# A two-layer encoder on one core: first norm's weights loaded by themselves, x's operands rounded straight from x, first weight bases split by DMA

## The chip, the cores and the metric

The kernel runs on one NeuronCore of one Trainium2 chip. The metric is the device time of one execution in microseconds (us). All work is float32. TensorE multiplies operands of type fp32r, a rounded float32; to keep the precision each operand is split into a high part (the value rounded to fp32r) and a low part (the value less its high part), and each product is made as high x high, high x low and low x high: three matmuls where one would do.

## What is computed

Two layers of a Conformer-like trunk over 528 tokens (16 meta tokens and 512 of the sequence), width 1024. Only the first part of the first layer matters here:

```
x = x + 1/2 * SwiGLU_1(RMSNorm(x))          # ffn1_norm, ffn1_w_in, ffn1_w_out
h = RMSNorm(x); proj = h @ w_in             # conv branch | attention | gates
x = x + W_out(sigmoid(g_A) * y_A + sigmoid(g_B) * y_B)
x = x + 1/2 * SwiGLU_2(RMSNorm(x))

def rms_norm(x, g):
    return x * rsqrt(mean(x * x) + EPS) * g
def swiglu(h, w_in, w_out):
    gu = h @ w_in
    gate, up = gu[..., :D_FF], gu[..., D_FF:]
    return (silu(gate) * up) @ w_out
```

## The kernel before

Everything is kept transposed: features on the 128 partitions, tokens along the free axis. x is `resid`, eight blocks (m = 0 to 7) of 128 features by 528 tokens.

**The product of an FFN's first stage.** The 2816 gate and 2816 up columns are cut into 22 "pairs" j, each 128 gate and 128 up columns. A pair is multiplied by a Strassen-like scheme in seven products P1 to P7 instead of eight. `seventh` (L1125) makes one product: 12 matmuls of 264 columns, in steps kp = 0 to 3. The other side of the products are seven operands made from two x blocks at a time (m = 2kp and 2kp + 1, each in halves of 264 tokens, times the norm's weight): B11, B21, B22 are such halves themselves, and T1 to T4 are sums and differences of them. Their high parts stand in `x7h`, their low parts in `x7l`. A pair's weights arrive in `raw` (SyncE's queue, `load_pair`: 768 KB, then 256 KB). Of them two tiles ("A", 128x1024) and one tile ("A22", 128x512) are used as they are: these are the **bases**. Four more tiles are sums (`sum12`, `sum43`), which VectorE adds. High parts of weights are in `wha`/`whb`, low parts in `wla`/`wlb`.

**How weights are split.** Sums, in all pairs, are rounded on ScalarE (`sum_hi`, L709) and subtracted on VectorE (`sum_lo`, L1537). The bases of pairs 2 and up: ScalarE rounds (`base_hi`, L687; `base22_hi`, L698) and writes the negative of the rounded part into the low buffer (L691, L702), and then a DMA on GpSimd's queue adds the weights from memory onto it (`accum_op=ALU.add`, L617 and L622). The bases of pair 0 and A of pair 1 are rounded on ScalarE too, but subtracted on VectorE (`first_base_lo`, L1553), which counts `first_lo`; A22 of pair 1 goes the way of the later ones.

**The order of work at the begin.** Each engine has its instructions in an order written out by hand, and waits on semaphores. ScalarE issues the loads of all parameters (`prm`, 312 KB, L668, and two small ones), waits for them, and then goes through the x blocks (`x7_parts`): L758 writes x times the weight as float32 into a scratch buffer (`tmp` or a part of `ga`), L769 squares x for the norm's statistic, L766 and L772 round the operands. VectorE (`x7_operands`) makes the sums T1 to T4 from the scratch (L1494 to L1503) and the low parts (L1489). TensorE waits for the first base (`first_lo`), then alternates between the statistic (`first_stat`, L1145: a product of ones with the squares, four records a block) and P1's steps; after that come P2, P5, P6, P3 of pair 0 and P1, P2 of pair 1. The squares have four buffers, so that the square of block m > 3 waits until the statistic of block m - 4 is done (`sq_used`). After the opening ScalarE copies banks (L724, L729, L734) and VectorE takes the gate sum (`gate_sum`, L1626) of pair 0, and goes on with pair 1's sums.

Of the kernel before, what the change touches and what calls it, by code (L numbers as in the profile page):

```python
# [25 lines left out]
ACT = mybir.ActivationFunctionType  # L26
# [237 lines left out]
def build(nc, x, params, qk_gain, sinks, pairs, outs6, outs5, mixes, out):  # L264
# [7 lines left out]
    with ctx:  # L272
# [26 lines left out]
        gnext = sb("gnext", [P, KD])  # L299
        qk = sb("qk", [HD, 4])  # L300
# [163 lines left out]
        prm_in, first_lo, sq_used = sem("prm_in"), sem("first_lo"), sem("sq_used")  # L464
# [74 lines left out]
        def _(sp):  # L539
# [4 lines left out]
            def load_pair(j):  # L544

                j0, j1 = run_of(j)
                if j - 2 >= j0:
                    sp.wait_ge(a_hi, j - 1)
                    sp.wait_ge(s_sum, 4 * (j - 1))
                if j in (2, 3):  # L550

                    sp.wait_ge(first_lo, 2 * j - 3)
                sp.dma_start(raw[:, j % 2, KP:4 * KP, :], pairs[j, :, KP:4 * KP, :]).then_inc(raw_in[j % 2], 16)
                if j - 2 >= j0:
                    sp.wait_ge(a22_hi, j - 1)
                if j == 2:
                    sp.wait_ge(first_lo, 2)
                sp.dma_start(raw[:, j % 2, 0:KP, :], pairs[j, :, 0:KP, :]).then_inc(raw22_in[j % 2], 16)
# [26 lines left out]
            load_pair(1)  # L585
            for l in range(DEPTH):
# [26 lines left out]


# [50 lines left out]
        def _(act):  # L665
            func = nc.scalar.activation

            act.dma_start(prm[:, :, :], params).then_inc(prm_in, 16)  # L668
            act.dma_start(qk[:, :], qk_gain).then_inc(par_in, 16)
            act.dma_start(sink[:, :, :, :], sinks).then_inc(par_in, 16)  # L670
# [10 lines left out]
            def base_hi(j):  # L681
# [6 lines left out]
                if j < 2:  # L688
                    return
                act.wait_ge(a_hi, j + 1)  # L690
                func(units(lo_units, U_A[REGION[j]], 2), hi.bitcast(F32), ACT.Copy, scale=-1.0).then_inc(a_neg, 1)  # L691

            def base22_hi(j):
# [5 lines left out]
                if j == 0:  # L699
                    return  # L700
                act.wait_ge(a22_hi, j + 1)
# [44 lines left out]

            def x7_parts(l, which, s, m, gain):
# [6 lines left out]
                if s:  # L754
                    act.wait_ge(acc_done, (n - 1) * (KD + 2) + m + 1)
                if m > (1 if s else 3):
                    act.wait_ge(x7_lo, X7_PARTS * (k - (s == 0)) - 1)
                func(tmp[:, 3 * w:5 * w] if odd else tmp[:, 6 * w:8 * w], resid[:, m, a:], ACT.Identity,  # L758
                     scale=gain).then_inc(b_done, 1)
                if odd:  # L760
                    act.wait_ge(b_done, s * KD + m + 1)

                    n = 2 if s else 4
                    if s == 0:
                        act.wait_ge(t_step, 4 * k + 1)
                    func(x7h[:, kp, 0:n * w], tmp[:, 3 * w:(3 + n) * w], ACT.Copy).then_inc(x7_hi, n // 2)  # L766
                if s == 0 and m > 3:
                    act.wait_ge(sq_used, m - 3)
                func(sq_m[:, m % 2, a:] if s else first_sq(m), resid[:, m, a:], ACT.Square).then_inc(x_sq, 1)  # L769
# [3 lines left out]
                elif s:  # L773
                    act.wait_ge(t_step, 4 * k + 1)
                    func(x7h[:, kp, 2 * w:4 * w], tmp[:, 5 * w:7 * w], ACT.Copy).then_inc(x7_hi, 1)
# [112 lines left out]
            act.wait_ge(prm_in, 16)  # L888
            for m in range(KD):
                act.wait_ge(x_in[m], 16)  # L890
                x7_parts(0, 0, 0, m, prm[:, m, R_FFN1 * DEPTH:R_FFN1 * DEPTH + 1])
                if m == 1:
                    base_hi(0)
                if m == 3:
                    base22_hi(0)
                if m == 5:
                    sum_hi(0, 0)
            sum_hi(0, 1)
            base_hi(1)
# [191 lines left out]
        def _(pe):  # L1091
# [67 lines left out]
            def last_product(j):  # L1159
                pe.wait_ge(*((a22_lo[j % 2], 16 * ((j + 1) // 2)) if j else (first_lo, 2)))  # L1160
# [21 lines left out]
            def ffn(l, f):  # L1182
                s, which = 2 * l + f, 2 * f
                for c, (ta, tb) in enumerate(CHUNKS):
# [10 lines left out]
                    for j in range(j0, j1):  # L1195
# [6 lines left out]
                        pe.wait_ge(*((a_lo[j % 2], 16 * (j // 2)) if j > 1 else (first_lo, 2 * j + 1)))  # L1202
# [244 lines left out]
        def _(dve):  # L1447
# [27 lines left out]

            def x7_operands(l, which, s, m):
# [16 lines left out]
                if not odd:  # L1493
                    tt(t1, b11, b12, ALU.subtract).then_inc(t_step, 1)  # L1494
                    if s:
                        add_squares(n, m, a)
                        low(1, T1, 5, 2)
# [6 lines left out]
                low(2, B21, 3, 2 if s else 4)  # L1504
                if s:
                    add_squares(n, m, a)
# [49 lines left out]
            for k in range(KD):  # L1556
                x7_operands(0, 0, 0, k)
                if k == 1:
                    first_base_lo("A", 0)
                if k == 3:  # L1560
                    sum12(0)
                    sum43(0)
                if k == 5:
                    sum_lo(0, 0)
            sum_lo(0, 1)
            first_base_lo("A22", 0)
            first_base_lo("A", 1)
# [437 lines left out]
def laid_out(inputs):  # L2005
# [12 lines left out]
    for l in range(DEPTH):  # L2018
# [11 lines left out]
    return {  # L2030
        "x": tiles(np.concatenate([f["meta_tokens"], f["x"][0]])),
# [24 lines left out]
```

## Time and profile before

| | before |
|---|---|
| median of 3 runs | 2352.43 us |
| lowest and highest | 2347.88 and 2353.43 us |
| profiled execution, its own time | 2354.66 us |
| its span | 2352.8 us |
| TensorE busy | 2319.3 us, 99% of the span |
| VectorE, ScalarE, GpSimd busy | 71%, 53%, 15% |
| granted TensorE clock, mean | 0.999 |

The span is the time between the first and the last instruction of the profile; the profiled execution took 1.9 us more than its span. Every slice of a fortieth of the span but the first shows TensorE at 90% or more.

### The profile page before, as it was taken

The page shows a single profiled execution, that of the slowest core. Times are in us where ns is not written, and L with a number is a line of the kernel's source. Part 1 is how long each engine was busy: PE and PEld are TensorE (multiplying, and loading weights), DVE is VectorE, ACT ScalarE, POOL GpSimd, SP SyncE. Part 2 cuts the span into 40 slices and gives each one's busy share as a digit, 9 for nine tenths or more (in the row PEclk, how much of TensorE's full clock was granted, in tenths as well). Part 3 has the DMA queues.
Part 4 walks back from the last instruction along what each step waited for, and adds up shares of the span by engine and source line. Part 5 has one row for each costly group of instructions (what it writes and reads, how often), then busy time and mean ns, then how long its engine had stood idle before and what let it go on. Part 6 is the DMA issues. An engine that isn't in the chain of part 4 may idle for free.

```text
span 2352.8 us, 43248 instructions
## 1 busy us (share of the span) xinstructions
PE 2319.3 (99%) x17765; PEld 2202.2 (94%) x17765; DVE 1678.4 (71%) x2751; ACT 1246.6 (53%) x2023; POOL 345.9 (15%) x454
## 2 busy tenths in 40 slices
PE   7999999999999999999999999999999999999999
PEld 6999999999999999999999999999888777998997
DVE  8855854899995488568677558548999755874773
ACT  8734734454445486356577357344544455862751
POOL 1101101112112211011011011012122122110110
PEclk9999999999999999999999999999999999999999
DMA  6845736677768968467458467366777698773753
GB/s 179 183 121 140 172 93 149 150 155 157 149 136 206 205 140 180 113 147 181 117 139 186 113 146 170 88 152 150 163 163 152 136 220 186 161 181 102 171 132 110
DMA packets 111365, 358.71 MB, mean 152 GB/s; under 512 B 12608, under 2 KB 12608, under 8 KB 111168
## 3 DMA queue, kind: packets, MB, share of 16 engines
q0 software_dynamic: 64080, 210.53, 44.1%
q1 hardware_dynamic: 46720, 145.08, 21.2%
q8 instruction: 141, 2.31, 0.4%
q14 instruction: 56, 0.46, 0.1%
q10 hardware_dynamic: 368, 0.33, 0.0%
HBM read 351.41 MB, written 2.10 MB: 150 GB/s over the span
## 4 chain that ended last, share of the span: by engine, by line
PE 83%; DVE 8%; DMA 4%; ACT 3%; issue 2%; DVEq 0%; ACTq 0%; SPq 0%
PE po L1108 26%; PE po L1125 21%; PE po L1176 21%; PE ptr L1125 7%; PE pov L1125 5%; DVE cv L1776 3%; DMA wha<-in_mixes 1%; DMA raw<-in_pairs 1%; DMA wla<-in_mixes 1%; PE pov L1368 1%; PE pov L1371 1%; PE pstat L1328 1%; DVE t L1817 1%; PE ptr L1337 1%; ACT whb L687 0%
## 5 line engine op out<-in xcount | busy, mean ns | idle before, releaser
L1108 PE MATMUL po<-xh,wha 128*128 128x264 f32 (+1 forms) x1408 | 346.9, 313 | 2.1 <-DMA wla<-in_mixes 1.6
L1108 PE MATMUL po<-xl,wha 128*128 128x264 f32 (+1 forms) x1408 | 335.8, 305 | 0.0
L1108 PE MATMUL po<-xh,wla 128*128 128x264 f32 (+1 forms) x1408 | 335.1, 305 | 0.0
L1776 DVE SCALAR_TENSOR_TENSOR cv<-ub,lp,cv 128x528 f32<-128x528 f32 (+1 forms) x480 | 333.2, 752 | 1.7
L1176 PE MATMUL po<-hh,wla 128*128 128x264 f32 (+1 forms) x1232 | 283.8, 300 | 0.0
L1176 PE MATMUL po<-hl,wha 128*128 128x264 f32 (+1 forms) x1232 | 283.7, 300 | 0.0
L1176 PE MATMUL po<-hh,wha 128*128 128x264 f32 (+1 forms) x1232 | 282.5, 299 | 0.4 <-DVE wla L1545 0.4
L678 ACT ACTIVATE wla<-wha 128x1024 fp32r<-128x1024 f32 x136 | 143.8, 1059 | 231.2 <-DMA wha<-in_mixes 231.0
L1545 DVE TENSOR_TENSOR wla<-wfa,wha 128x768 fp32r<-128x768 f32 (+1 forms) x128 | 113.8, 890 | 203.8 <-ACT wha L716 203.7
L1108 PEld LDWEIGHTS po<-xh,wha 128*128 128x128 f32 x1408 | 227.1, 189 | 24.3 <-issue 7.3
L716 ACT ACTIVATE wha<-wfa 128x768 fp32r<-128x768 f32 (+1 forms) x128 | 101.0, 789 | 268.8 <-DMA wfa<-in_outs 268.7
L1108 PEld LDWEIGHTS po<-xh,wla 128*128 128x128 f32 x1408 | 226.5, 188 | 11.2
L1108 PEld LDWEIGHTS po<-xl,wha 128*128 128x128 f32 x1408 | 226.9, 188 | 9.8
L1125 PE MATMUL po<-x7h,wha 128*128 128x264 f32 (+1 forms) x832 | 236.0, 284 | 0.0
L1125 PE MATMUL po<-x7h,wla 128*128 128x264 f32 (+1 forms) x832 | 236.0, 284 | 0.0
L1125 PE MATMUL po<-x7l,wha 128*128 128x264 f32 (+1 forms) x832 | 236.0, 284 | 0.0
L1125 PE MATMUL po<-x7h,whb 128*128 128x264 f32 (+1 forms) x768 | 220.5, 287 | 6.3 <-ACT tmp L729 3.4
L1125 PE MATMUL po<-x7l,whb 128*128 128x264 f32 (+1 forms) x768 | 218.2, 284 | 0.0
L1125 PE MATMUL po<-x7h,wlb 128*128 128x264 f32 (+1 forms) x768 | 217.7, 283 | 0.0
L1176 PEld LDWEIGHTS po<-hh,wha 128*128 128x128 f32 x1232 | 196.1, 188 | 8.5 <-DVE wla L1545 0.6
L1176 PEld LDWEIGHTS po<-hh,wla 128*128 128x128 f32 x1232 | 196.9, 189 | 7.5
L1176 PEld LDWEIGHTS po<-hl,wha 128*128 128x128 f32 x1232 | 196.4, 188 | 7.5
(251 smaller groups left out, 5659.1 us busy)
## 6 DMA issues: line engine op xcount, KB each, us to landing
wha<-in_mixes POOLq DMA_DIRECT2D x136, 512.0 KB, 4.4
wla<-in_mixes POOLq DMA_DIRECT2D x136, 512.0 KB, 6.8
raw<-in_pairs SPq DMA_DIRECT2D x88, 768.0 KB, 5.6
wfa<-in_outs SPq DMA_DIRECT2D x64, 384.0 KB, 3.1
wlb<-in_pairs POOLq DMA_DIRECT2D x47, 512.0 KB, 8.4
raw<-in_pairs SPq DMA_DIRECT2D x88, 256.0 KB, 6.9
wla<-in_pairs POOLq DMA_DIRECT2D x87, 256.0 KB, 6.6
wfa<-in_outs SPq DMA_DIRECT2D x64, 320.0 KB, 2.9
```

What stands on the lines that cost most here:

```text
L678: func(mix_units(lo_units, n), mix_units(hi_units, n).bitcast(F32), ACT.Copy, scale=-1.0)\
L716: func(units(hi_units, u, 2)[:, 0:k, :], units(f32_units, u, 2)[:, 0:k, :], ACT.Copy).then_inc(ob_hi, 1)
L1108: ins = mm(po[:, 2 * out_slot + h, 0:width], w[:, k, :], v[:, k, t:t + width], start=begin and k == 0 and p == 0, stop=last and k == kt - ...
L1125: ins = mm(bank, a[:, kp, :], b[:, kp, cols7], start=begin and kp == 0 and p == 0, stop=kp == KP - 1 and p == 2, skip_group_check=True)
L1176: ins = mm(po[:, 2 * ps(m) + h, 0:width], w[:, k, :], v[:, t, x:x + width], start=t == 0 and p == 0, stop=t == CHUNK_T - 1 and p == 2, ski ...
L1328: ins = mm(score(i, h), q[r, :], kw[r, c:c + WK], start=True, stop=True)
L1337: ins = tr(ptr[:, (2 * n + h) * P:(2 * n + h + 1) * P], pw[:, (b + 1) % 2, at:at + WIN], ident[:, :])
L1368: mm(dst[h * HD:(h + 1) * HD], vw[:, pos - 1, :], cut(pt[:, i, h, :]), start=True, stop=False, skip_group_check=True)
L1371: ins = mm(dst[h * HD:(h + 1) * HD], vz[0:n, i - i0, h, :], cut(ptm[0:n, :]), start=pos == 0, stop=True, skip_group_check=True)
L1545: tt(units(lo_units, u, 2)[:, 0:k, :], units(f32_units, u, 2)[:, 0:k, :], units(hi_units, u, 2)[:, 0:k, :].bitcast(F32), ALU.subtract).the ...
L1776: stt(cv[:, j, a:], u, w, cv[:, j, a:], ALU.mult, ALU.add).then_inc(conv_step, 1)
L1817: nc.vector.reciprocal(t0[0:HD, :], t0[0:HD, :]).then_inc(krms_ready, 1)
```

## The change

It touches the first some thirty microseconds of the program, and nothing after pair 3's loads. (1) The first norm's weight is an input of its own, `first_gain`, 128x8 elements; ScalarE loads it first, and the loads of all parameters move to SyncE's queue, behind pair 1's. (2) `x7_parts` and `x7_operands` give way, in the first stage, to `first_parts` and `first_operands`: B11, B21 and B22 are rounded straight from `resid` with the weight as scale, without a copy in the scratch (only B12 is written there), and VectorE takes their low parts and the sums from `resid` too, with a negated weight `nfgain`. (3) The bases of pair 0 and A of pair 1 are not rounded on ScalarE or subtracted on VectorE: a DMA on GpSimd's queue loads the weights into the high buffer, rounding on the way (`first_load`), ScalarE writes the negative (`first_base_neg`), and a second DMA adds the weights (`first_add`). (4) SyncE's waits for pairs 2 and 3 drop what hung on `first_lo`.

```
+            firsts = ((0, U_A, 2, KP, 3 * KP), (0, U_A22, 1, 0, KP), (1, U_A, 2, KP, 3 * KP))
+            def first_load(i):
+                j, u, n, a, z = firsts[i]
+                pool.dma_start(units(hi_units, u[REGION[j]], n), pairs[j, :, a:z, :]).then_inc(first_hi[i], 16)
+            def first_add(i):
+                j, u, n, a, z = firsts[i]
+                pool.wait_ge(first_neg, i + 1)
+                pool.dma_start(units(lo_units, u[REGION[j]], n), pairs[j, :, a:z, :], accum_op=ALU.add)\
+                    .then_inc(first_lo[i], 16)
+            first_load(0)
+            pool.wait_ge(x_in[3], 16)
+            first_load(1)
+            first_add(0)
+            pool.wait_ge(x_in[6], 16)
+            first_load(2)
+            first_add(1)
+            first_add(2)
...
-            act.dma_start(prm[:, :, :], params).then_inc(prm_in, 16)
-            act.dma_start(qk[:, :], qk_gain).then_inc(par_in, 16)
-            act.dma_start(sink[:, :, :, :], sinks).then_inc(par_in, 16)
+            act.dma_start(fgain[:, :, :], first_gain).then_inc(gain_in, 16)
...
+            def first_base_neg(i):
+                j, u, n = ((0, U_A, 2), (0, U_A22, 1), (1, U_A, 2))[i]
+                act.wait_ge(first_hi[i], 16)
+                func(units(lo_units, u[REGION[j]], n), units(hi_units, u[REGION[j]], n).bitcast(F32), ACT.Copy,
+                     scale=-1.0).then_inc(first_neg, 1)
+            def first_squares(m):
+                if m > 3:
+                    act.wait_ge(sq_used, m - 3)
+                func(first_sq(m), resid[:, m, :], ACT.Square).then_inc(x_sq, 1)
+            def first_parts(kp):
+                tmp, w = x7_scratch(0, kp), NH
+                e, o = 2 * kp, 2 * kp + 1
+                act.wait_ge(x_in[e], 16)
+                if kp > 1:
+                    act.wait_ge(x7_lo, X7_PARTS * (kp - 1) - 1)
+                func(tmp[:, 7 * w:8 * w], resid[:, e, w:2 * w], ACT.Identity, scale=fgain[:, e, :]).then_inc(b_done, 2)
+                func(x7h[:, kp, B11 * w:(B11 + 1) * w], resid[:, e, 0:w], ACT.Identity, scale=fgain[:, e, :])
+                first_squares(e)
+                act.wait_ge(t_step, 4 * kp + 1)
+                func(x7h[:, kp, T1 * w:(T1 + 1) * w], tmp[:, 5 * w:6 * w], ACT.Copy).then_inc(x7_hi, 1)
...
-            act.wait_ge(prm_in, 16)
...
+            act.wait_ge(gain_in, 16)
+            first_parts(0)
+            first_base_neg(0)
+            first_parts(1)
+            first_base_neg(1)
+            first_parts(2)
+            sum_hi(0, 0)
+            first_parts(3)
             sum_hi(0, 1)
-            base_hi(1)
+            first_base_neg(2)
...
-                        pe.wait_ge(*((a_lo[j % 2], 16 * (j // 2)) if j > 1 else (first_lo, 2 * j + 1)))
+                        pe.wait_ge(*((a_lo[j % 2], 16 * (j // 2)) if j > 1 else (first_lo[2 * j], 16)))
...
-            def first_base_lo(part, j):
-                a, z, first_unit, n = (KP, 3 * KP, U_A, 2) if part == "A" else (0, KP, U_A22, 1)
-                dve.wait_ge(a_hi if part == "A" else a22_hi, j + 1)
-                u = first_unit[REGION[j]]
-                tt(units(lo_units, u, n), raw[:, j, a:z, :], units(hi_units, u, n).bitcast(F32), ALU.subtract)\
-                    .then_inc(first_lo, 1)
```

GpSimd's queue, from its last instruction of the constants on. Before:

```order
L610 AFFINE_SELECT ident<-ident 128x128
L617 DMA wlb<-in_pairs 128x1024 [waits a_neg]
L622 DMA wla<-in_pairs 128x512 [waits a22_neg]
L617 DMA wla<-in_pairs 128x1024 [waits a_neg]
L622 DMA wla<-in_pairs 128x512 [waits a22_neg]
```

And with the change:

```order
L613 AFFINE_SELECT ident<-ident 128x128
L622 DMA whb<-in_pairs 128x1024
L622 DMA wha<-in_pairs 128x512 [waits x_in3]
L627 DMA wlb<-in_pairs 128x1024 [waits first_neg]
L622 DMA wha<-in_pairs 128x1024 [waits x_in6]
L627 DMA wla<-in_pairs 128x512 [waits first_neg]
L627 DMA wla<-in_pairs 128x1024 [waits first_neg]
L641 DMA wlb<-in_pairs 128x1024 [waits a_neg]
L646 DMA wla<-in_pairs 128x512 [waits a22_neg]
```

Six transfers now stand ahead of pair 2's addition. The one that ends in `wlb` is pair 0's A, behind the load of A22, which waits for x block 3; the last `first_neg` one is pair 1's A.

ScalarE, from the first use of x blocks 2 and 3 to the negative or rounding of A22. Before:

```order
L687 ACTIVATE whb<-raw 128x1024 [waits raw_in0]
L758 ACTIVATE ga<-resid,prm 128x528 [waits x_in2]
L769 ACTIVATE ga<-resid 128x528
L758 ACTIVATE ga<-resid,prm 128x528 [waits x_in3]
L766 ACTIVATE x7h<-ga 128x1056 [waits t_step,b_done]
L769 ACTIVATE ga<-resid 128x528
L772 ACTIVATE x7h<-ga 128x792 [waits t_step]
L698 ACTIVATE wha<-raw 128x512 [waits raw22_in0]
```

And with the change:

```order
L768 ACTIVATE wlb<-whb 128x1024 [waits first_hi0]
L783 ACTIVATE ga<-resid,fgain 128x264 [waits x_in2]
L784 ACTIVATE x7h<-resid,fgain 128x264
L774 ACTIVATE ga<-resid 128x528
L787 ACTIVATE x7h<-ga 128x264 [waits t_step]
L789 ACTIVATE x7h<-resid,fgain 128x528 [waits x_in3]
L774 ACTIVATE ga<-resid 128x528
L793 ACTIVATE x7h<-ga 128x792 [waits t_step]
L768 ACTIVATE wla<-wha 128x512 [waits first_hi1]
```

The two full-width copies into the scratch became one of half the width, and the instruction on the weights reads what a DMA wrote instead of `raw`.

ScalarE, from block 7's square on to the first bank copy. Before:

```order
L769 ACTIVATE ga<-resid 128x528 [waits sq_used]
L772 ACTIVATE x7h<-ga 128x792 [waits t_step]
L709 ACTIVATE whb<-wfb 128x1024 [waits s_sum]
L687 ACTIVATE wha<-raw 128x1024 [waits raw_in1]
L724 ACTIVATE tmp<-po 128x264 [waits t_step,c12_taken,blk_used]
```

And with the change:

```order
L774 ACTIVATE ga<-resid 128x528 [waits sq_used]
L793 ACTIVATE x7h<-ga 128x792 [waits t_step]
L727 ACTIVATE whb<-wfb 128x1024 [waits s_sum]
L768 ACTIVATE wla<-wha 128x1024 [waits first_hi2]
L742 ACTIVATE tmp<-po 128x264 [waits t_step,c12_taken,blk_used]
```

The negative of pair 1's A stands in the place of its rounding, at the end of the opening, and the addition of pair 1's A waits for it.

## Rows read from the trace of the kernel before

**Rows 1.** Busy time by stretches: opening, two pairs, rest, first transfers.

```profile
0.00:11.45 11.45, 0.67 (x4) 0.62 (x4) 5.36 (x13) 8.01 (x12) 0.91 (x9) 1.00 0.86 305
11.45:31.20 19.75, 17.46 (x91) 14.72 (x92) 18.97 (x29) 17.73 (x25) 0.00 (x0) 1.00 0.32 108
31.20:52.90 21.70, 19.82 (x160) 19.24 (x158) 21.23 (x32) 17.66 (x26) 3.75 (x5) 1.00 0.71 160
52.90:2352.80 2299.90, 2281.37 (x17514) 2167.61 (x17514) 1632.84 (x2680) 1203.20 (x1963) 341.26 (x441) 1.00 0.66 152
4.00:14.00 10.00, 2.55 (x6) 2.04 (x7) 7.38 (x12) 8.99 (x13) 0.00 (x0) 1.00 1.03 400
```

**Rows 2.** Timeline of TensorE: start, duration, idle before with its releaser.

```profile
11.45 3.89 PE L1145 MATMUL pstat<-ga,ones 128*128 128x264 f32 x8 [9.00 <-DVE wlb L1553]
...
15.69 1.94 PE L1145 MATMUL pstat<-ga,ones 128*128 128x264 f32 x8
...
20.17 1.16 PE L1145 MATMUL pstat<-ga,ones 128*128 128x264 f32 x4 [1.28 <-ACT ga L769]
...
28.28 0.39 PE L1125 MATMUL po<-x7h,whb 128*128 128x264 f32 x1 [0.67 <-ACT tmp L724]
...
35.14 0.36 PE L1125 MATMUL po<-x7h,whb 128*128 128x264 f32 x1 [0.73 <-DVE tmp L1630]
...
49.31 0.39 PE L1125 MATMUL po<-x7h,whb 128*128 128x264 f32 x1 [0.74 <-ACT tmp L724]
...
52.89 0.36 PE L1125 MATMUL po<-x7h,whb 128*128 128x264 f32 x1 [0.40 <-ACT tmp L729]
```

**Rows 3.** Timeline of ScalarE, the same columns.

```profile
4.84 0.73 ACT L758 ACTIVATE tmp<-resid,prm 128x528 f32<-128x528 f32 x1 [0.96 <-DMA prm<-in_params]
5.48 0.63 ACT L769 ACTIVATE ga<-resid 128x528 f32<-128x528 f32 x1
...
8.34 0.85 ACT L772 ACTIVATE x7h<-tmp 128x792 fp32r<-128x792 f32 x1
9.09 1.04 ACT L687 ACTIVATE whb<-raw 128x1024 fp32r<-128x1024 f32 x1
10.04 0.72 ACT L758 ACTIVATE ga<-resid,prm 128x528 f32<-128x528 f32 x1
...
26.91 1.04 ACT L687 ACTIVATE wha<-raw 128x1024 fp32r<-128x1024 f32 x1
27.86 0.37 ACT L724 ACTIVATE tmp<-po 128x264 f32<-128x264 f32 x1
```

**Rows 4.** Timeline of VectorE, the same columns.

```profile
28.18 1.82 DVE L1553 TENSOR_TENSOR wla<-raw,wha 128x512 fp32r<-128x512 f32 x2
29.92 0.43 DVE L1626 TENSOR_TENSOR tmp<-pov,tmp 128x264 f32<-128x264 f32 x1
```

**Rows 5.** The issues of x blocks 2 and 3: duration, first and last start, landing.

```profile
L542 SPq DMA_DIRECT2D resid<-in_x x2: 480/568/657, 2.6 to 3.3; - x2
...
DMA to landing us min/median/max: 6.4/6.4/6.4
```

**Rows 6.** Adding transfers of 512 KB, whole run: issue ns, landing.

```profile
L617 POOL DMA_DIRECT2D wlb<-in_pairs x47: 861/866/1014, 32.9 to 2261.4; - x47
L617 POOL DMA_DIRECT2D wla<-in_pairs x39: 859/866/889, 47.0 to 2251.7; - x39
...
DMA to landing us min/median/max: 5.4/8.5/12.0
```

**Rows 7.** The first of them, issued at 32.9, in the same columns.

```profile
L617 POOL DMA_DIRECT2D wlb<-in_pairs x1: 1014/1014/1014, 32.9 to 32.9; - x1
...
DMA to landing us min/median/max: 8.6/8.6/8.6
```

**Rows 8.** The mixer's plain rounding loads of 512 KB, whole run.

```profile
L627 POOL DMA_DIRECT2D wha<-in_mixes x136: 543/546/868, 320.0 to 1979.4; - x136
...
DMA to landing us min/median/max: 3.7/4.4/9.4
```

More of the change, by code:

```diff
@@ L261, in block_source, with build @@
     return "w_in", (({A: 0, B: O_B, GA: O_GA, GB: O_GB}[kind] + j * P, P),)
-def build(nc, x, params, qk_gain, sinks, pairs, outs6, outs5, mixes, out):
+def build(nc, first_gain, x, params, qk_gain, sinks, pairs, outs6, outs5, mixes, out):
     rows = lambda w: w.rearrange("l (k p) n -> p l k n", p=P)
@@ L463, in build @@
         raw_in, raw22_in = [sem(f"raw_in{s}") for s in range(2)], [sem(f"raw22_in{s}") for s in range(2)]
-        prm_in, first_lo, sq_used = sem("prm_in"), sem("first_lo"), sem("sq_used")
+        prm_in, sq_used = sem("prm_in"), sem("sq_used")
+        gain_in, gain_neg = sem("gain_in"), sem("gain_neg")
+        first_hi, first_lo = [sem(f"first_hi{i}") for i in range(3)], [sem(f"first_lo{i}") for i in range(3)]
+        first_neg = sem("first_neg")
         a_hi, a_neg, a_lo = sem("a_hi"), sem("a_neg"), [sem(f"a_lo{s}") for s in range(2)]
@@ L585, in _ @@
             load_pair(1)
+            sp.dma_start(prm[:, :, :], params).then_inc(prm_in, 16)
+            sp.dma_start(qk[:, :], qk_gain).then_inc(par_in, 16)
+            sp.dma_start(sink[:, :, :, :], sinks).then_inc(par_in, 16)
             for l in range(DEPTH):
@@ L761, in x7_parts @@
                     act.wait_ge(b_done, s * KD + m + 1)
[L763 to L769, printed above, removed]
+                    func(x7h[:, kp, 0:2 * w], tmp[:, 3 * w:5 * w], ACT.Copy).then_inc(x7_hi, 1)
+                func(sq_m[:, m % 2, a:], resid[:, m, a:], ACT.Square).then_inc(x_sq, 1)
                 if odd:
@@ L1494, in x7_operands @@
                     tt(t1, b11, b12, ALU.subtract).then_inc(t_step, 1)
-                    if s:
-                        add_squares(n, m, a)
-                        low(1, T1, 5, 2)
+                    add_squares(n, m, a)
+                    low(1, T1, 5, 2)
                     return
@@ L1503, in x7_operands @@
                 stt(t4, t2, -1.0, b21, ALU.mult, ALU.subtract).then_inc(t_step, 1)
-                low(2, B21, 3, 2 if s else 4)
-                if s:
-                    add_squares(n, m, a)
+                low(2, B21, 3, 2)
+                add_squares(n, m, a)
                 low(3, T3, 0, 3)
@@ L1546, in out_lo @@
                    units(hi_units, u, 2)[:, 0:k, :].bitcast(F32), ALU.subtract).then_inc(ob_lo, 1)
-            def first_base_lo(part, j):
-                a, z, first_unit, n = (KP, 3 * KP, U_A, 2) if part == "A" else (0, KP, U_A22, 1)
-                dve.wait_ge(a_hi if part == "A" else a22_hi, j + 1)
-                u = first_unit[REGION[j]]
-                tt(units(lo_units, u, n), raw[:, j, a:z, :], units(hi_units, u, n).bitcast(F32), ALU.subtract)\
-                    .then_inc(first_lo, 1)
[L1556 to L1564, printed above, removed]
+            dve.wait_ge(gain_in, 16)
+            ts(nfgain[:, :, :], fgain[:, :, :], -1.0, None, ALU.mult).then_inc(gain_neg, 1)
+            dve.wait_ge(gain_neg, 1)
+            first_operands(0)
+            first_operands(1)
+            sum12(0)
+            sum43(0)
+            first_operands(2)
+            sum_lo(0, 0)
+            first_operands(3)
             sum_lo(0, 1)
-            first_base_lo("A22", 0)
-            first_base_lo("A", 1)
             def layer_params(l):
```

68 lines of the change are left out of this document (40 added, 28 removed).

## The prediction

> **What bounds the kernel now.** I read the busy time by stretches first, then the timelines of TensorE, ScalarE and VectorE over the opening, then the transfers. TensorE is busy 2281.4 of the 2299.9 us after 52.9 [rows 1]; nothing of the change reaches there, so the question is only when TensorE comes to the point that it reaches at 52.9 now. Before that it has 0.67 + 17.46 + 19.82 us of work [rows 1] and a begin at 11.45, when VectorE has subtracted the first base [rows 2]. From there the reader is to see two things. First, TensorE has idle time of 2.3 us up to 31.2 (19.75 less 17.46) and 1.9 us more in three waits, 0.73, 0.74 and 0.40, up to 52.9 [rows 1, 2], because ScalarE and VectorE feed it just in time: ScalarE works without a gap from 26.91 to its bank copy at 27.86 [rows 3], and VectorE takes the gate sum at 29.92 only because the last two base subtractions fill 28.18 to 30.0 [rows 4]. Second, the transfers are the busiest part of the begin: from 4 to 14 us they move 400 GB/s at a busy share of 1.03 [rows 1]. So a gain would have to come from the 11.45 us of the start or the 4.2 us of idle; the whole stake is a few us of 2352.
>
> **What the change removes.** (a) ScalarE's wait for the parameters, 0.96 us before 4.84 [rows 3]. It can begin at 3.9 at the earliest, as its table load and constant end there, and it needs x block 0; I take 4.3, a gain of 0.5. (b) ScalarE's work per pair of x blocks. Now it takes 4.25 us (4.84 to 9.09, rounding of the base not included) [rows 3]. After: two 264-wide pieces at some 0.4, two squares at 0.54 (the distance of the starts; one lasts 0.63), a 264-wide copy 0.3 (the bank copy lasts 0.37), a 528-wide piece 0.64, the 792-wide copy 0.75, together 3.5 to 3.6. Four times 0.7 is 2.8 us. (c) On VectorE the base subtractions: 1.2 us after the first pair (as one half of L1553's kind) and the 1.8 at 28.18 [rows 4], 3 us; its sums and low parts cost the same, cut differently. These gains are real only where ScalarE and VectorE set the pace.
>
> **What it adds, and this decides.** TensorE's begin waited for a subtraction; now it waits for a chain through GpSimd's queue. All of TensorE's opening is queued behind that one wait: the statistic, P1, and through the four buffers of the squares ScalarE's block 4 and all behind it.
> - The load of pair 0's A goes out at about 1.7. The mixer's loads of that size land after 3.7 to 9.4 us, median 4.4 [rows 8]; so it lands at 6 to 11. ScalarE is done with pair 0 of x at 4.3 + 3.5 = 7.8; the negative (1.06, as the rounding of that size) ends at 9 to 12.
> - But the addition stands behind the load of A22, which waits for x block 3. That was issued at 3.3 and landed 6.4 later, at 9.7 [rows 5]. In flight ahead of it are now 512 KB more and 312 KB fewer; 0.2 MB at 400 GB/s is 0.5 us: 10.2. The A22 load's issue takes 0.87 (as each on that queue [rows 6]): the addition goes out at 11.1.
> - It lands 5.4 to 12.0 us later, median 8.5 [rows 6]; the first one of the run, issued while a pair's load was in flight, took 8.6 [rows 7]. At 11.1 some 1.5 to 2 MB of SyncE's transfers are still to come, so the quiet end, 5.4, is unlikely. I take 8.6: **T0 = 19.7**, against 11.45.
>
> The Trainium skill's page "DMA: Bandwidth & Descriptors" ("Anatomy of one DMA — SWDGE (gpsimd) path") gives a transfer from this queue as about 2.0 us plus the bytes at 436 GB/s. For 512 KB that would be 3.2 us, and T0 = 14.3. No row of this kernel comes near it: the fastest addition of 86 took 5.4 [rows 6], and not one plain load of 136 under 3.7 [rows 8].
>
> **From T0 on.** TensorE needs 17.5 us of work to the first product of pair 1 (busy time of 11.45 to 31.2 [rows 1]; its eight slow first records, 3.89 against 1.94 for the next eight [rows 2], are in it and stay, as it is idle before). Are its operands there? Pairs 0 and 1 of x are ready before T0. For the rest ScalarE waits until the statistic of block 0 is done, four slow records, T0 + 1.95. Then: square 0.54, copy 0.3, 0.64, to T0 + 3.45; block 5's square after the statistic of block 1 at T0 + 3.9; 0.54, 0.75, the rounded sum 0.95: T0 + 6.15. Pair 3: 3.6, and 0.4 for VectorE's first sum, which stands behind a low part: T0 + 10.15; second sum: 11.1; the negative of pair 1's A: T0 + 12.2. VectorE ends half a us behind the sum. TensorE needs pair 3's operands at T0 + 13, so it runs without the old 2.3 us of idle.
>
> Pair 1's A is the next thing late: its addition goes out at T0 + 12.2 and TensorE wants it at T0 + 17.5. At 32 us pair 2 has landed and pair 3 is not asked for, so the queue is quiet; between 5.4 and 8.6 I take 6: T0 + 18.2 = 37.9, a wait of 0.7, and the product starts 6.7 us later than at 31.2. If it takes 8.6, the wait is 3.3.
>
> Up to 52.9 the old waits of 1.9 us can give some back: 4.8 later. But the chain over ScalarE and VectorE, which made these waits, is late as well. P2 of pair 0 is done 2.9 us (P6, P3) before T0 + 17.5, the bank copies take 0.4 to 0.7, so the gate sum comes at T0 + 15.1 = 34.8, 4.9 later than 29.92. Behind the copies ScalarE has its table load and square root (2 us), which ended under VectorE's work before and now half come after it: some 0.5. Both ways give 4.8 to 5.4. **Sum: 5.4 us later**, all of it at the begin. The profiled execution took 2354.66, and would take 2360.1; the median of the runs is 2.2 lower, so 2357.8.
>
> The edits at nothing: the parameters' load behind pair 1's is wanted only by the layer's parameters, which VectorE takes among the first output blocks, behind eleven pairs; the work of these hides it, and it would cost only if it came later than they end. SyncE's dropped waits bring pair 2's A22 some 12 us earlier, which nobody waits for. The negated weight is eight elements on VectorE, under 0.2 us, before x.
>
> **The rivals.**
> - *As forecast*, T0 at 17.5 to 20.7: 2 to 7 us later. Chance 0.55.
> - *The transfers crowd each other more.* The addition takes 9.8 to 12, or x block 3 lands at 11 to 12 because two queues share the engines, or pair 1's addition takes the full 8.6 too. The last alone adds 2.6 less what the idle time takes, 1.5; each us of the first two adds one. 7.1 to 10 us later, 2359.5 to 2362. For it speaks that 4 to 14 us are full already [rows 1]; against it that x's first blocks are already out. Chance 0.24.
> - *The additions are quick*, 3.2 to 5.4 (the page's rule, or the lowest of [rows 6]): T0 = 14.3 to 16.5. Then all is shifted 5.4 to 3.2 less: 0 to 2.2 us later, 2352.4 to 2354.6. Chance 0.14.
> - *Faster*: the lighter opening of ScalarE and VectorE decides. That needs T0 under 14.3, the point where 2.9 us of later begin is paid by the 2.3 idle and 0.5 of the gate sum. With T0 at 12.5 it is 1.8 us faster, 2350.6; the most that ScalarE's 3.3 and VectorE's 3 us allow is 3 to 4. Against it stands that the addition goes out at 11.1 by block 3's landing alone, so it would have to land in 1.4 to 3 us. Chance 0.07, nearly all of it within 0.3%.
>
> **How the numbers follow.** 0.3%, 7.1 us here, is about what a measurement of this kernel can tell from no change; its three runs lie 5.5 us apart. The likeliest is 2357.8; its own range is 2354.4 to 2359.5. With the crowded case up to 10 us and half of the quick one, and the spread of the median by one or two us, the range for 8 in 10 is 2352.0 to 2361.8. Slower by over 0.3% is the crowded case, 0.24; faster by over 0.3% would need a gain beyond the whole idle time, 0.03; the rest, 0.73, is within.
>
> **What would show it.** In the changed profile: TensorE's first statistic at 18 to 21, released by the addition into `wlb` (step T0); ScalarE's square of block 4 waiting several us for TensorE (the buffers); TensorE without waits of over 0.5 us from there to pair 1, then a wait at its first product for a transfer into `wla` (0.7); the gate sum at 34 to 36; and the steady stretch beginning at 57 to 59 instead of 52.9. It is wrong if the addition lands within 5 us, if x block 3 lands well before 9.7, or if a wait remains behind 60 us that is not in the old trace.

## The result: 5.2 to 9.6 us slower, all of it at the begin

| | before | after |
|---|---|---|
| median of six runs each | 2352.2 us | 2360.67 us |
| lowest and highest | 2347.88 and 2353.43 | 2357.28 and 2364.96 |
| ratio after/before, 95% interval | | 1.0032 (1.0022 to 1.0041) |
| profiled execution, its own time | 2354.66 us | 2361.2 us |
| its span | 2352.8 us | 2359.4 us |
| TensorE busy | 2319.3 us, 99% | 2320.2 us, 98% |
| VectorE busy | 1678.4 us | 1678.0 us |

The interval is 5.2 to 9.6 us of 2352.2 us. The spans of the profiled executions lie 6.6 us apart and their times 6.5. Here is the changed kernel's busy time by stretches, in the columns of [rows 1]: stretch, length, busy time and count of TensorE, its weight loads, VectorE, ScalarE and GpSimd, then the granted TensorE clock, the transfers' busy share and GB/s.

```profile
0.00:21.55 21.55, 0.67 (x4) 0.61 (x4) 13.07 (x30) 11.34 (x20) 4.47 (x14) 1.00 0.95 306
21.55:39.59 18.04, 17.50 (x93) 15.43 (x93) 12.21 (x20) 13.61 (x21) 0.87 (x1) 1.00 0.41 94
39.59:59.37 19.78, 19.30 (x156) 19.11 (x157) 19.07 (x29) 16.95 (x25) 3.58 (x5) 1.00 0.77 176
59.37:2359.40 2300.03, 2282.70 (x17514) 2169.34 (x17514) 1633.66 (x2679) 1203.04 (x1963) 340.83 (x441) 1.00 0.66 152
4.00:14.00 10.00, 0.00 (x0) 0.00 (x0) 5.97 (x13) 6.91 (x14) 1.46 (x2) 1.00 1.01 357
```

The row to read first is the fourth. From 59.37 to the end it is 2300.03 us; before, from 52.9 to the end, it was 2299.90 [rows 1]. In these two executions the program behind the begin took the same time within 0.2 us, and the 6.5 us by which 52.89 became 59.37 are all but 0.1 us of the difference of the spans. The second row is the opening from TensorE's first statistic to the first product of pair 1: 17.50 us of work in 18.04 us, where before it was 17.46 in 19.75. The idle time is gone, but the stretch begins 10.1 us later.

TensorE's timeline (start, duration, instruction, in brackets the idle time before it and what released it) has three rows that count:

```profile
21.55 3.89 PE L1185 MATMUL pstat<-ga,ones 128*128 128x264 f32 x8 [19.10 <-DMA wlb<-in_pairs]
...
39.59 0.39 PE L1165 MATMUL ptr<-x7h,wha 128*128 128x264 f32 x1 [0.54 <-DMA wla<-in_pairs]
...
59.37 0.36 PE L1165 MATMUL po<-x7h,whb 128*128 128x264 f32 x1 [0.48 <-DVE wla L1598]
```

They answer to 11.45, 31.2 and 52.89 in [rows 1, 2]. The first release is no longer a subtraction on VectorE but a transfer into `wlb`, and the second is a transfer into `wla`. GpSimd's timeline shows what they hang on:

```profile
1.92 0.70 POOL L622 DMA_DIRECT2D whb<-in_pairs  x1 [0.24 <-issue]
12.42 0.54 POOL L622 DMA_DIRECT2D wha<-in_pairs  x1 [9.80 <-DMA resid<-in_x]
12.95 0.92 POOL L627 DMA_DIRECT2D wlb<-in_pairs  x1
...
34.04 0.87 POOL L627 DMA_DIRECT2D wla<-in_pairs  x1 [14.05 <-ACT wla L768]
```

The addition of pair 0's A stands behind the load of A22, and this behind the 9.80 us for x block 3. ScalarE, the same view:

```profile
3.74 0.51 ACT L783 ACTIVATE tmp<-resid,fgain 128x264 f32<-128x264 f32 x1 [1.05 <-DMA fgain<-in_first_gain]
...
10.37 1.06 ACT L768 ACTIVATE wlb<-whb 128x1024 fp32r<-128x1024 f32 x1 [2.95 <-DMA whb<-in_pairs]
...
23.71 0.64 ACT L774 ACTIVATE ga<-resid 128x528 f32<-128x528 f32 x1 [4.07 <-PE pstat L1185]
...
32.70 1.04 ACT L768 ACTIVATE wla<-wha 128x1024 fp32r<-128x1024 f32 x1
```

ScalarE begins 1.1 us earlier than before, and then stands 2.95 us for the load and 4.07 us for TensorE, which has not freed the squares' buffers. Last, the issues of x blocks 2 and 3, in the columns of [rows 5], and then the addition into `wlb`, in those of [rows 7]:

```profile
L546 SPq DMA_DIRECT2D resid<-in_x x2: 432/449/466, 2.6 to 3.1; - x2
...
DMA to landing us min/median/max: 8.9/9.0/9.0
```

```profile
L627 POOL DMA_DIRECT2D wlb<-in_pairs x1: 923/923/923, 13.0 to 13.0; - x1
...
DMA to landing us min/median/max: 8.6/8.6/8.6
```

The addition took the 8.6 us that were forecast. Block 3 did not land as forecast: it was issued at 3.1 and landed 9.0 us later, at 12.1 and not at 10.2.

### The profile page after: what moved, and what is told of

It reads as the page before. It is cut to its first block, busy times and chain, and to the rows that moved or that the text cites. A ratio compares the mean times of both kernels' runs of the same rounds, so it can differ in the third digit from the quotient of the medians.

```text
span 2359.4 us, 43254 instructions
## 1 busy us (share of the span) xinstructions
PE 2320.2 (98%) x17765; PEld 2204.5 (93%) x17765; DVE 1678.0 (71%) x2757; ACT 1244.9 (53%) x2027; POOL 349.7 (15%) x460
## 4 chain that ended last, share of the span: by engine, by line
PE 83%; DVE 8%; DMA 4%; ACT 3%; issue 2%; SPq 0%; POOL 0%; DVEq 0%; ACTq 0%
PE po L1148 25%; PE po L1165 22%; PE po L1216 21%; PE ptr L1165 7%; PE pov L1165 5%; DVE cv L1828 3%; DMA wha<-in_mixes 1%; DMA wla<-in_mixes 1%; PE pov L1408 1%; PE pov L1411 1%; PE pstat L1368 1%; DVE t L1869 1%; PE ptr L1377 1%; ACT pw L950 0%; ACT wla L700 0%
```

## The experiments

All times by label stand in one table. "First" is TensorE's first statistic, "gate" the start of VectorE's gate sum of pair 0, "last wait" the start of the instruction behind the last wait of the opening (52.89 before), "rest" the span less that, "raw A" the time from the issue of SyncE's load of pair 0's A (at 1.7) to its landing, "GB/s" what all transfers moved from 4 to 8 us. The ratio of each experiment is taken to runs of the kernel before from the same rounds, whose medians were 2353.54 us (e1 to e4), 2353.10 (e5 to e8) and 2354.18 (e9), and not to the 2352.2 of the first row.

| kernel | first | gate | last wait | rest | raw A | GB/s | median, us | ratio to before (95%) |
|---|---|---|---|---|---|---|---|---|
| before | 11.45 | 29.92 | 52.89 | 2299.9 | 6.0 | 383 | 2352.2 | |
| after | 21.55 | 36.16 | 59.37 | 2300.0 | 7.9 | 304 | 2360.67 | 1.0032 (1.0022 to 1.0041) |
| e1_old_split | 11.65 | 30.37 | 53.03 | 2299.8 | 7.6 | 253 | 2354.61 | 1.0004 (0.9995 to 1.0013) |
| e2_only_split | 19.86 | 33.50 | 60.57 | 2301.4 | 6.9 | 372 | 2359.58 | 1.0026 (1.0016 to 1.0036) |
| e3_add_first | 19.98 | 34.41 | 58.17 | 2302.2 | 8.6 | 291 | 2361.48 | 1.0033 (1.002 to 1.0045) |
| e4_stat_first | 5.20 | 34.87 | 57.88 | 2299.5 | 8.6 | 248 | 2359.2 | 1.0021 (1.0012 to 1.0029) |
| e5_prm_act | 10.22 | 28.95 | 51.61 | 2304.6 | 6.1 | 387 | 2352.95 | 1.0002 (0.9993 to 1.0011) |
| e6_mixed | 11.26 | 28.83 | 51.49 | 2302.5 | 7.2 | 291 | 2353.14 | 0.9997 (0.9987 to 1.0006) |
| e7_mixed_prm_act | 10.30 | 27.86 | 50.54 | 2300.6 | 5.9 | 388 | 2352.16 | 0.9997 (0.9988 to 1.0006) |
| e8_weight_alone | 11.46 | 30.35 | 53.34 | 2301.4 | 7.4 | 263 | 2355.58 | 1.001 (1.0001 to 1.0019) |
| e9_x_act | 10.99 | 28.55 | 51.22 | 2302.4 | 6.9 | 374 | 2354.96 | 1.0004 (0.9995 to 1.0014) |

Two columns help to read the others. The rest goes from 2299.5 to 2304.6 us by the profiled execution, over instructions that no edit touched; so the time of one execution cannot tell two kernels 2 us apart, and the ratios, with intervals 4 us wide, hardly can, and the begin is judged by the columns up to "last wait". These and the next two come from one execution of each kernel. How far they can be trusted is seen where two kernels run the same program up to 8 us: e1 and e6 read 7.6 and 7.2 us for raw A and 253 and 291 GB/s, and the changed kernel, e3 and e4 read 7.9, 8.6 and 8.6 us and 304, 291 and 248 GB/s. And from the gate sum to the last wait it is 22.7 to 23.8 us in all kernels but e2. What counts is when VectorE takes the gate sum.

### e1: the change with the old way of splitting

```
-            first_load(0)
...
-            first_add(2)
...
+                src = raw[:, j, 0:KP, :] if i == 1 else raw[:, j, KP:3 * KP, :]
+                func(units(hi_units, u[REGION[j]], n), src, ACT.Copy).then_inc(first_neg, 1)
...
             first_operands(0)
+            first_base_lo(0)
...
             sum_lo(0, 1)
+            first_base_lo(1)
+            first_base_lo(2)
```

ScalarE rounds the three bases from `raw` again and VectorE subtracts; parts (1) and (2) of the change stay.

> The changed kernel with its DMA split of the three first bases undone: ScalarE rounds them from raw and VectorE subtracts, as before; the weight by itself and the operands straight from x stay. If the additions on GpSimd's queue are the whole loss (my theory), TensorE begins at about 10 us instead of 21.6, and the gain of the rest of the change appears: VectorE, with some 23.7 us of work from 4.4 on, comes to its gate sum at about 28 instead of 29.9, and TensorE's steady stretch begins near 51 (52.9 before, 59.4 with the change); time 1 to 3 us under before. If the operands straight from x are a loss of their own (the rival), the steady stretch begins after 53 and the time is not under before.

The last wait ends at 53.03, 6.3 us before that of the changed kernel. So the split by transfers is what costs. But the other half of the expectation failed, and its rival's sign, a steady stretch after 53, is there: the rest of the change, which takes some 2.3 us of work off ScalarE (pair 0 of x takes 3.68 us instead of 4.25, four times), brings nothing (53.03 against 52.89). TensorE begins at 11.65 and not at 10, since the raw weights land 1.6 us later than before; e5 takes that up. For the work behind it VectorE shows the reason. First e1 from its first subtraction to the gate sum, then the low parts in e1's opening grouped by shape (count, busy time, mean ns of one, idle time before):

```profile
10.38:30.37 19.99, 16.88 (x83) 14.22 (x84) 19.81 (x33) 16.58 (x29) 0.00 (x0) 1.00 0.39 144
```

```profile
L1531 DVE SCALAR_TENSOR_TENSOR x7l<-resid,fgain,x7h 128x528 fp32r<-128x528 f32 x4 | 3.0, 762 | 0.0
...
L1528 DVE SCALAR_TENSOR_TENSOR x7l<-resid,fgain,x7h 128x264 fp32r<-128x264 f32 x4 | 2.0, 489 | 0.0
...
L1520 DVE SCALAR_TENSOR_TENSOR tmp<-resid,fgain,tmp 128x264 f32<-128x264 f32 x2 | 1.0, 490 | 0.5 <-ACT tmp L779 0.5
...
L1529 DVE TENSOR_TENSOR x7l<-tmp,x7h 128x264 fp32r<-128x264 f32 x2 | 0.9, 426 | 0.0
```

And the kernel before over the same piece, and its low parts and sums by shape:

```profile
10.17:29.92 19.75, 16.18 (x81) 13.44 (x82) 19.00 (x29) 17.73 (x26) 0.00 (x0) 1.00 0.35 123
```

```profile
L1489 DVE TENSOR_TENSOR x7l<-tmp,x7h 128x1056 fp32r<-128x1056 f32 x2 | 2.5, 1260 | 0.1
...
L1494 DVE TENSOR_TENSOR tmp<-tmp 128x264 f32<-128x264 f32 x2 | 0.9, 429 | 4.3 <-ACT tmp L758 4.3
```

VectorE is busy 19.81 of 19.99 us in e1: it sets the length of this piece, and ScalarE's lighter work buys nothing. Nor did VectorE itself get lighter. Per pair of x blocks its four sums took 4 x 0.43 and the first low part 1.26, 2.98 us. Now the sums take 4 x 0.49 (they multiply by the weight on the way), and that low part is cut in three, 0.49 + 0.43 + 0.76: 3.64 us. The 0.66 us more, four times, are 2.6 us, which is what the changed kernel gave back of the 3.1 us of the three subtractions it dropped. Its total says so: 1678.0 us against 1678.4.

### e2: the kernel before with the split alone

```
+            first_load(0)
+            pool.wait_ge(x_in[3], 16)
+            first_load(1)
+            first_add(0)
+            pool.wait_ge(x_in[6], 16)
+            first_load(2)
+            first_add(1)
+            first_add(2)
...
-                    base_hi(0)
+                    first_base_neg(0)
...
-                    first_base_lo("A", 0)
```

> The kernel before with the DMA split of the three first bases alone. If the additions are the whole loss, TensorE's first statistic comes at 21.5 to 22.5 and the steady stretch begins at 59 to 61, 6 to 8 us over before. If part of the loss comes from the operands straight from x, it begins at 56 or earlier.

The split alone puts the last wait 7.7 us later (60.57), and the total does not contradict it (1.0026, up to 1.0036). TensorE's timeline:

```profile
19.86 3.88 PE L1166 MATMUL pstat<-ga,ones 128*128 128x264 f32 x8 [17.42 <-DMA wlb<-in_pairs]
...
39.26 0.39 PE L1146 MATMUL ptr<-x7h,wha 128*128 128x264 f32 x1 [2.86 <-DMA wla<-in_pairs]
```

It begins 1.7 us before the changed kernel, and before the 21.5 that was expected (block 3 landed at 11.4, and the addition took 7.6 us). The wait for pair 1's A, 2.86 us, takes most of this back: it is the second wait for a transfer that the forecast named, and pair 1 starts at 39.26, still 0.3 us before the changed kernel's 39.59. From there to the last wait, however, it is 21.31 us instead of 19.78. This is the clock. Behind the long wait the matmuls start 0.12 us apart up to 40.6 and then 0.22 us apart up to 44.0, fifteen of them, 1.5 us more than at full speed, and the row of this stretch shows a granted clock of half:

```profile
40.90:44.00 3.10, 3.10 (x16) 3.10 (x15) 1.49 (x3) 2.78 (x4) 0.86 (x1) 0.50 0.91 170
```

In the changed kernel, which waited 0.54 us there, and in e3, which waited 1.08, the same piece takes 19.78 and 19.77 us. So a transfer that TensorE waits for can cost more than the wait.

### e3: the first addition ahead of A22's load

```
             first_load(0)
+            first_add(0)
             pool.wait_ge(x_in[3], 16)
             first_load(1)
-            first_add(0)
```

> The changed kernel with the addition onto pair 0's A issued before the load of A22, so that it does not wait for x block 3. If every us of the addition's landing is a us of the end, it goes out at 11.5 instead of 12.95, lands after the same 8.6, TensorE begins at 20.1 and the steady stretch at 57.9 instead of 59.4. If the transfers in flight set the landing and not the issue (rival), the addition takes as much longer as it goes out earlier, and nothing moves.

The addition now waits only for the negative, and goes out at 11.86 instead of 12.95:

```profile
11.86 0.87 POOL L627 DMA_DIRECT2D wlb<-in_pairs  x1 [9.25 <-ACT wlb L768]
```

The first statistic came 1.57 us earlier and the last wait ended 1.2 us earlier; pair 1's A took 0.5 back (a wait of 1.08 instead of 0.54). So the queue's order costs about 1 us, and most of the loss is the addition itself, which took 8.1 us here. The rival, that the landing would not move, is out. The total (1.0033) cannot tell this from the changed kernel.

### e4: the statistic before the wait for the base

```
-                        pe.wait_ge(*((a_lo[j % 2], 16 * (j // 2)) if j > 1 else (first_lo[2 * j], 16)))
+                        if j:
+                            pe.wait_ge(*((a_lo[j % 2], 16 * (j // 2)) if j > 1 else (first_lo[2], 16)))
...
                                     first_stat(2 * kp + 1)
+                                    if kp == 0:
+                                        pe.wait_ge(first_lo[0], 16)
```

> The changed kernel with TensorE's wait for pair 0's A moved behind the statistic of x blocks 0 and 1. If TensorE's work behind T0 is what the begin consists of, its 3.9 us of slow first statistic fall into the wait, and the steady stretch begins near 55.5 instead of 59.4; ScalarE's square of block 4 then waits for nothing. If the slow records only move to the products behind the wait, as TensorE is idle again for 10 us, a part of the 3.9, up to 2, is not gained.

The first eight statistic records left the chain, and ScalarE's square of block 4 waits for nothing, as expected; but the last wait ends only 1.5 us earlier, at 57.88, less than the 2 us that the expectation left at the worst. TensorE's timeline behind its wait:

```profile
21.88 0.59 PE L1165 MATMUL po<-x7h,whb 128*128 128x264 f32 x1 [12.80 <-DMA wlb<-in_pairs]
22.27 0.42 PE L1165 MATMUL po<-x7l,whb 128*128 128x264 f32 x1
22.49 0.42 PE L1165 MATMUL po<-x7h,wlb 128*128 128x264 f32 x1
22.71 3.72 PE L1185 MATMUL pstat<-ga,ones 128*128 128x264 f32 x8
...
29.34 0.29 PE L1165 MATMUL po<-x7l,whb 128*128 128x264 f32 x1
29.47 0.29 PE L1165 MATMUL po<-x7h,wlb 128*128 128x264 f32 x1
```

At 22.27 the matmuls start 0.22 us apart, at 29.34 0.13. 264 columns in 0.22 us is 1.2 GHz, the lower of the clock's two levels. TensorE had stood idle for 12.80 us before. Starting the statistic early did not spare the slow stretch, it made a second one: eight records took 3.89 us at 5.20 and the next eight 3.72 at 22.71, where the changed kernel's second eight take 2.64. The first product starts 2.98 us earlier than there (21.88 against 24.86), and the last step of P1 is done only 1.29 us earlier (29.59 against 30.88, the start of `pov`).

### e5 and e8: where the parameters' load stands

e5 is e1 with the parameters' loads back on ScalarE's queue, behind the first weight's; e8 is the kernel before with part (1) of the change alone.

```
             act.dma_start(fgain[:, :, :], first_gain).then_inc(gain_in, 16)
+            act.dma_start(prm[:, :, :], params).then_inc(prm_in, 16)
+            act.dma_start(qk[:, :], qk_gain).then_inc(par_in, 16)
+            act.dma_start(sink[:, :, :, :], sinks).then_inc(par_in, 16)
```

> The kernel of e1_old_split (DMA split undone, the rest of the change kept) with the loads of all parameters back on ScalarE's queue, behind that of the weight. There, and with the change, pair 0's A landed in raw at 9.3 to 9.6 us and the transfers moved 220 to 300 GB/s from 4 to 8 us, where before and in e2_only_split, with these loads on ScalarE's queue, it landed at 7.7 to 8.6 and 300 to 430 GB/s moved. If that queue's place is the cause, it lands at 7.7 to 8 here, ScalarE rounds it at 7.5 to 8 instead of 9.29, TensorE begins at 10 to 10.4 instead of 11.65 and the gate sum comes 1 to 1.4 us earlier, at about 29.1; steady stretch at 51.8. If the order of the inputs in memory or something else is the cause, it lands at 9 or later and nothing moves.

e8 takes from the kernel before the waits and loads of the parameters on ScalarE:

```
-            act.dma_start(prm[:, :, :], params).then_inc(prm_in, 16)
...
+            act.dma_start(fgain[:, :, :], first_gain).then_inc(gain_in, 16)
...
-                x7_parts(0, 0, 0, m, prm[:, m, R_FFN1 * DEPTH:R_FFN1 * DEPTH + 1])
+                x7_parts(0, 0, 0, m, fgain[:, m, :])
```

> The kernel before with the first part of the change alone: the first norm's weight loaded by itself, all parameters on SyncE's queue behind pair 1's. ScalarE begins at 3.7 instead of 4.84. If the raw transfer is slower without the parameters on ScalarE's queue, pair 0's A lands at 9.3, TensorE begins at 11.6 and the steady stretch at 53 as before: the us won at the start is lost again. If not, TensorE begins at 10.4 and the steady stretch at 51.8.

First e1's stretch from 4 to 8 us, and then its load of pair 0's A in the columns of [rows 5] (the landing is that of this load and the one behind it):

```profile
4.00:8.00 4.00, 0.00 (x0) 0.00 (x0) 3.70 (x8) 3.32 (x7) 0.00 (x0) 1.00 0.89 253
```

```profile
L557 SPq DMA_DIRECT2D raw<-in_pairs x1: 424/424/424, 1.7 to 1.7; - x1
...
DMA to landing us min/median/max: 7.6/7.7/7.8
```

And the same two of e5:

```profile
4.00:8.00 4.00, 0.00 (x0) 0.00 (x0) 3.08 (x7) 3.99 (x10) 0.00 (x0) 1.00 1.03 387
```

```profile
L557 SPq DMA_DIRECT2D raw<-in_pairs x1: 426/426/426, 1.7 to 1.7; - x1
...
DMA to landing us min/median/max: 6.1/6.2/6.4
```

With the parameters' 312 KB on a second queue, pair 0's A landed 1.5 us earlier, though more bytes were asked for at that time. The last wait ended at 51.61, 1.4 us before e1's. e8 is the other side: ScalarE starts at 3.67 instead of 4.84, but raw A lands 1.4 us later, and nothing is won (53.34 against 52.89; by the total it is the slower one, 1.0010, with an interval that just leaves out 1). The rates in the table have no exception. With the parameters on ScalarE's queue (before, e2, e5, e7) the transfers move 372 to 388 GB/s from 4 to 8 us; without them (after, e1, e3, e4, e6, e8) 248 to 304. From 8 to 14 us it is 388 to 411 GB/s in all of them.

### e6 and e7: each base by the way that suits it

```
-            first_load(0)
             pool.wait_ge(x_in[3], 16)
             first_load(1)
-            first_add(0)
...
             first_parts(1)
-            first_base_neg(1)
             first_parts(2)
+            first_base_neg(1)
             sum_hi(0, 0)
+            first_base_neg(2)
             first_parts(3)
             sum_hi(0, 1)
-            first_base_neg(2)
...
             first_operands(0)
+            first_base_lo()
```

In e6 pair 0's A, which TensorE wants first, is rounded and subtracted on the engines; A22 of pair 0 and A of pair 1, wanted 17 us later or more, go by transfers, and their negatives are written earlier. e7 is e6 with the parameters back on ScalarE's queue.

> The changed kernel with pair 0's A alone rounded on ScalarE and subtracted on VectorE as before; pair 0's A22 and pair 1's A keep the load and the addition by DMA, with their negatives moved ahead of the rounded sum and of x blocks 6 and 7. If the loss is the first addition in TensorE's way and nothing else of the split, TensorE begins at 11.7 as in e1_old_split, VectorE has 1.75 us less work than there (a 512 and a 1024 wide subtraction), and the gate sum comes at 28.6 instead of 30.37, the steady stretch at 51.6 (52.9 before, 59.4 with the change). If the transfers by themselves hurt (x late, additions late), TensorE waits for pair 1's A or for x and the steady stretch begins after 53.

> The kernel of e6_mixed with the loads of all parameters on ScalarE's queue. The best of what these runs point to: if both reasons hold, TensorE begins at 10 to 10.4, the gate sum comes at 27.5 to 28 and the steady stretch begins at 50.5 to 51, 2 us earlier than before; the time is 1 to 3 us under before, which the intervals may not tell from none.

All came as expected. The gate sum came at 28.83 in e6, 1.54 us before e1's, of which 0.4 is the earlier landing of the raw weights, which its edit cannot explain. In e7 it came 0.97 earlier again, at 27.86. e7's timeline of TensorE:

```profile
10.30 3.88 PE L1189 MATMUL pstat<-ga,ones 128*128 128x264 f32 x8 [7.85 <-DVE wlb L1616]
...
50.54 0.36 PE L1169 MATMUL po<-x7h,whb 128*128 128x264 f32 x1 [0.38 <-ACT tmp L747]
```

Its begin is 2.35 us shorter than before's. The total is not resolved: 0.9997 with an interval of 0.9988 to 1.0006, in which 2.35 us (0.9990) lies near the lower end. No kernel here is shown to beat the one before by its total time.

### e9: x blocks on the second queue instead of the parameters

```
             act.dma_start(fgain[:, :, :], first_gain).then_inc(gain_in, 16)
+            for k in (2, 3):
+                act.dma_start(resid[:, k, :], x[:, k, :]).then_inc(x_in[k], 16)
...
-            for k in range(2, KD):
+            for k in range(4, KD):
```

> The kernel of e6_mixed with the loads of x blocks 2 and 3 on ScalarE's queue, behind that of the weight, and the parameters left on SyncE's. It asks what it is in the parameters' place that makes pair 0's A land 1.5 us earlier. If any larger transfer on a second queue keeps the rate up, 4 to 8 us show about 390 GB/s as with the parameters there (291 in e6_mixed), all the more bytes having been moved, pair 0's A lands at 8 or earlier (8.85 in e6_mixed) though 528 KB more are in flight beside it, and blocks 2 and 3 by 7. If it is the parameters' transfer itself or where it lies in memory, the rate stays under 310, and pair 0's A lands after 9, behind blocks 2 and 3.

Two x blocks on ScalarE's queue bring the rate to 374 GB/s as well (e6: 291), so it is not the parameters' own transfer that matters. But the rest of the expectation failed. Raw A landed 6.9 us after its issue, at 8.6, which is 0.3 better than in e6 and within the 0.4 by which e1 and e6 differ without a reason; block 3 landed at 8.8 and not by 7; and the last wait moved by 0.27 us. The blocks were also issued earlier, at 1.2 and 1.7 instead of 2.6 and 3.1, so that this run does not tell a second queue from an earlier issue. An early issue alone is not enough: the changed kernel, e3 and e4 put 512 KB on GpSimd's queue at 1.9 and stay at 304 GB/s or less.

## Why the forecast came out as it did

**That the chain through GpSimd's queue decides: right, shown from both sides.** Without it 6.3 us are gone (e1), with it alone 7.7 are there (e2).

**T0 = 19.7: the one large miss, measured 21.55.** It lies beyond the 18 to 21 that the forecast named. Its terms in turn: ScalarE began 1.1 us earlier, not 0.5, at 3.74 and so before the 3.9 that was taken for the earliest, and ended pair 0 at 7.4 (7.8 forecast; 3.7 us of work, where 3.5 was forecast); the load landed 8.4 us after 1.92 (6 to 11), the negative ended at 11.4 (9 to 12); the A22 load's issue took 0.54, not 0.87; the addition took 8.6 (8.6). The step that failed is "0.2 MB at 400 GB/s is 0.5 us: 10.2", the landing of x block 3: 12.1. It counted bytes at the rate of before. From landing to the issue another 0.3 us passed, which the forecast had at nothing, and the shorter issue paid for it. Block 3 landed at 9.7 before, at about 11.4 with GpSimd's 512 KB beside (e2) and 11.2 with the parameters gone from the second queue (e1). Each of the two costs some 1.6 us alone, and both together 2.4: the load of 512 KB more, and a rate that fell from 383 to 304 GB/s because the 312 KB "fewer" had gone out early on ScalarE's queue. That the two queues crowd each other was in the rival of crowded transfers; that taking these loads off ScalarE's queue costs was in none.

**From T0 on: right within half a us.** 17.50 us of work (17.5), no wait on the way, the negative's addition out at T0 + 12.5 (12.2), landing after 5.5 (6), a wait of 0.54 (0.7), gate sum at T0 + 14.6 (15.1). ScalarE's wait for the squares' buffers was there too, 4.07 us.

**The sum, 5.4 us later: 6.5 measured in the profiled executions.** T0 was 1.85 late, 0.5 came back with the gate sum and 0.3 behind it. That lies in the likeliest case's 2 to 7, but its T0 does not, and the condition of the crowded rival, block 3 landing at 11 to 12, is what happened. By the medians, 8.5 us apart, the result falls into that rival's range (2359.5 to 2362), which had a chance of 0.24; the interval, 5.2 to 9.6 us, covers both, and does not decide whether the change is above or below 0.3% either. So the chain was right, and the size came out near partly because small errors behind T0 went the other way.

**From 6.5 to 8.5 us.** The forecast took 2.2 us off the profiled execution to come to a median; after the change this distance is 0.5. That accounts for most of the way from 2357.8 to 2360.67, and it is scatter of executions rather than the change: in the rounds of the experiments the unchanged kernel had medians of 2353.54, 2353.10 and 2354.18 us, and 2360.67 lies 6.5 to 7.6 us above these. No run shows a loss behind the begin.

**"Its sums and low parts cost the same, cut differently": wrong.** They cost 0.66 us more per pair of blocks, and VectorE's 3 us of savings were all but gone. It did not move the forecast, as behind T0 = 21.55 VectorE is busy only 12.21 of 18.04 us. It would have moved that of the rival "faster", which counted on 3 us there, and it is, beside the raw weights' later landing, why e1 disappointed.

**A quicker addition: not seen.** The Trainium skill's page "DMA: Bandwidth & Descriptors" ("Anatomy of one DMA — SWDGE (gpsimd) path") gives about 2.0 us and the bytes at 436 GB/s, an estimate of 3.2 us for a 512 KB transfer from this queue. The trace does not agree: the two loads of that size took 8.4 and 8.2 us at the begin, the additions 8.6 and, with little else moving, 5.5.

**Still open:** why the transfers move only 250 to 300 GB/s from 4 to 8 us when ScalarE's queue has no more than the weight's 4 KB, and whether it is the second queue or the earlier issue on it that helps.

## What to carry to other kernels

Handing an engine's work to a transfer pays where nobody waits for the result (e6, some 1.1 us of the begin) and costs where the first matmul waits for it: here 8.6 us of transfer replaced 1.2 us of subtraction. A long wait can cost again behind itself, by the clock (e2, 1.5 us behind 2.86). Before making an engine's work lighter, look which engine has no idle time in that stretch; ScalarE's 2.3 us were worth nothing beside a VectorE busy 19.81 of 19.99. And at the begin, where transfers are the busiest part, see on which queues they stand and not only how many bytes they move.

## What the runs showed of the hardware

**Loads on ScalarE's queue as well raise the rate at the begin.** Loads on SyncE's queue alone, or with GpSimd's beside them, moved 248 to 304 GB/s from 4 to 8 us; with 312 KB or two x blocks also on ScalarE's queue it was 372 to 388. With the parameters there the first weights land 1.3 to 1.5 us earlier (e5 against e1, e7 against e6, before against e8: 5.9 to 6.1 us after their issue against 7.2 to 7.6), and SyncE's six issues of x take 3.2 to 3.4 us instead of 4.2 to 4.8. With x blocks there they land 0.3 us earlier (e9 against e6), which is within the scatter. The Trainium skill's page "DMA: Bandwidth & Descriptors" ("Rules for kernel authors") says that spreading transfers over the engines' queues doesn't help bandwidth, as all run on the same sixteen DMA engines. In this stretch it did, at 387 against 253 GB/s (e5, e1), and with the same bytes in all at 374 against 291 (e9, e6). From 8 to 14 us, at 405 and 399 (e5, e1), the page and the runs agree.

**The granted clock of the rows can miss TensorE's half speed.** In e4 this row holds matmuls that start 0.22 us apart, behind 12.80 us of idle time, and reads 1.00:

```profile
21.88:25.00 3.12, 3.12 (x9) 2.60 (x10) 3.12 (x5) 3.08 (x6) 0.00 (x0) 1.00 1.04 319
```

In e2 the row from 40.90 to 44.00, with the same distance of 0.22 us behind 2.86 us of idle time, reads 0.50, and agrees. The distance between starts shows both, and is the thing to read after a long wait.

**A weight taken from memory costs VectorE something.** A `SCALAR_TENSOR_TENSOR` on 264 columns that multiplies by a per-partition weight took 0.49 us (e1, L1520 to L1528), one without such a weight 0.43 (before, L1501 and L1503).
